# A feed-forward up-projection on TensorE: seven half-size block products in place of eight for 19 of 22 feature tiles

## The chip, the cores and the metric

The kernel runs on one core of one Trainium2 chip. The metric is the device time of one execution in microseconds (us), the median over runs. TensorE (PE in the profile) multiplies, VectorE (DVE), ScalarE (ACT) and GpSimd (POOL) do elementwise work, and SyncE (SP) issues the DMAs.

## The reference, cut to what matters

Two layers, each a token mixer and then a gated feed-forward network (FFN), over 1024 tokens of 1024 features. Only the FFN changes, and in it the first matrix product:

```
def conv_ffn(x, w_in, b_in, conv_w, conv_b, w_out, b_out):
    h = x @ w_in + b_in                      # 1024 x 1024 by 1024 x 5632
    hp = jnp.pad(h, ((0, 0), (1, 1), (0, 0)))
    h = hp[:, :-2] * conv_w[0] + hp[:, 1:-1] * conv_w[1] + hp[:, 2:] * conv_w[2] + conv_b
    u, g = jnp.split(h, 2, axis=-1)          # 2816 features each: 22 tiles of 128
    return (u * jax.nn.gelu(g, approximate=False)) @ w_out + b_out
```

Everything is float32. The residual is added and the sum is layer-normalised.

## The kernel before

`build` runs five kinds of stage one after the other, with a barrier of all engines between them: attention, output projection (`output_stage`), FFN (`ffn_stage`, L968), neighbourhood attention, and again output projection and FFN. The FFN stage is run twice, once for each layer, from about 797 us to 1545 us and from about 2200 us to the end.

Precision: each float32 operand is split into a high part rounded to the fp32r type and a low part, the rest. A product is three matmuls: high by high, high by low, low by high. So one output bank of 128x512 takes 3 matmuls for each 128 of the inner dimension.

In `ffn_stage` the input X is held transposed as XTh and XTl: feature blocks k = 0 to 7 on partitions, 1024 tokens along the free dimension. The hidden features come in FT = 22 tiles f of 128, each in two parities: the value u (parity 0) and the gate g (parity 1). The pieces of work are:

* **Up tile** (`up_tile`, L1121, matmul L1131): for one f and one parity, 2 token halves x 8 k x 3 = 48 matmuls of 128x128 by 128x512 into PSUM `ph[parity]`.
* **Split** (`split`, L1064 to L1072, GpSimd): a 512 KB weight tile that a DMA has put into `wraw` is rounded to `wh` (L1069) and subtracted into `wl` (L1071). `hold` makes it keep order.
* **Take** (`take`, ScalarE): L1229 copies `ph` with bias into H, L1233 makes the centre tap of the convolution in C.
* **Conv** (VectorE): L1289 (left tap) and L1294 (right tap) add into C. Then `gate` (ScalarE, L1239, Gelu), product (VectorE, L1307), `high` (ScalarE, L1243) and `low` (VectorE, L1311) make the two parts Ah and Al of the activation.
* **Down** (`down`, L1134, matmul L1145): for two tiles f at once, 16 output banks r of 6 matmuls each, into four PSUM banks `po` in turn. VectorE adds each bank to X (L1282). TensorE waits before bank r until bank r - 4 has been added.

The order is written out by hand for each engine; the engines meet only at semaphores and each takes its own list in order. On TensorE: tiles of f = 0 and 1, then nine rounds of (both tiles of f = 2i+2, down(i), both tiles of f = 2i+3), then f = 20 and 21, then `down_four` (L1155), which does the last four f at once. Ahead of the rounds ScalarE rescales X (8 instructions, L1221) and GpSimd adds a bias to X (8 instructions, L1079), put between the splits. All VectorE instructions named conv, product, low read two operands from SBUF; the adds of L1282 read one from PSUM and one from SBUF.

Of the kernel before, what the change touches and what calls it, by code (L numbers as in the profile page):

```python
# [9 lines left out]

# [20 lines left out]
class Mem:  # L31
# [11 lines left out]
    def sb(self, name, shape, dt=F32):  # L43
        return self.ctx.enter_context(self.nc.sbuf_tensor(f"{self.prefix}_{name}", shape, dt))

# [649 lines left out]
class Norm:  # L695
# [9 lines left out]
    def __init__(self, nc, m, X, g, b, XTh, XTl, ident, turned_psum, finished):  # L705
# [3 lines left out]
        self.gb = m.sb("gb", [P, 2, self.D])  # L709
# [258 lines left out]
def ffn_stage(nc, name, w_in_d, b_in, conv_w, conv_b, w_out, b_out, g, b, x_out, X, XTh, XTl, ident, alpha, last_layer,  # L968
              wraw, WH, WL, next_tiles):
# [8 lines left out]
    KT, TT, FT = D // P, X.shape[1], FF // P  # L978
    S = TT * P
    G = FT // 2  # L980
    NT = 2 * FT
    with ExitStack() as ctx:  # L982
        m = Mem(nc, ctx, name)
        CUT = 2
        wh, wl = WH[:, 0:4], WL[:, 0:4]
        Ah, Al = WH[:, 4:8], WL[:, 4:8]
        prefetch = None if last_layer else Prefetch(m, wraw, next_tiles)
        H = m.sb("H", [P, 2, S + 2])
        C = m.sb("C", [P, 2, S])
        prow = m.sb("prow", [NT, 5, P])  # L990
        par = m.sb("par", [P, 5, NT])
        centre = m.sb("centre", [P, 2, NT])
        bias = m.sb("bias", [P, D])
        ph = [m.ps(f"ph{i}", [P, KT, P]) for i in range(2)]
        po = [m.ps(f"po{i}", [P, BANK]) for i in range(4)]
        FINISHED = (TT - 1,)
        norm = Norm(nc, m, X, g, b, XTh, XTl, ident, ph, FINISHED)
        wt_in = [m.sem(f"wt_in{i}") for i in range(2)]
        w_high, w_low = m.sem("w_high"), m.sem("w_low")
        par_in, par_turned, par_set, pads_set, bias_in = (m.sem(s) for s in ("par_in", "par_turned", "par_set", "pads_set", "bias_in"))  # L1000
        up_done, up_out, conv_link, conv_done, gated, prod_ready, a_high, a_low = (
            m.sem(s) for s in ("up_done", "up_out", "conv_link", "conv_done", "gated", "prod_ready", "a_high", "a_low"))
        down_done, added, pool_passed = m.sem("down_done"), m.sem("added"), m.sem("pool_passed")
        centre_step = m.sem("centre_step")
        rescaled, biased = m.sem("rescaled"), m.sem("biased")
        y_stored = [m.sem(f"y_stored{i}") for i in range(2)]
        block = ctx.enter_context(nc.Block())
        LAST_SLOTS = (1, 2, 0, 1, 2, 0, 3, 1)
        OUTS = TT * (D // BANK)
        EARLY = 8  # L1010

        def last_bank(r):

            return po[r % 4] if r < 4 or r >= EARLY else ph[(r - 4) // 2][:].rearrange("p k n -> p (k n)")[:, (r % 2) * BANK:(r % 2 + 1) * BANK]

        @block.sync
        def _(sp):
            sp.dma_start(prow[:, 0], b_in.rearrange("(t p) -> t p", p=P)).then_inc(par_in, 16)
            sp.dma_start(prow[:, 1:4], conv_w.rearrange("c (t p) -> t c p", p=P)).then_inc(par_in, 16)
            sp.dma_start(prow[:, 4], conv_b.rearrange("(t p) -> t p", p=P)).then_inc(par_in, 16)  # L1020

            def up(w, slot, f, gate, first=False):
                if not first:
                    sp.wait_ge(w_low, w - 1 - CUT)
                sp.dma_start(wraw[:, slot].rearrange("p (k n) -> p k n", k=KT),
                             column_tile(w_in_d, f * P + gate * FF)).then_inc(wt_in[slot], 16)

            def down(w, slot, f):
                sp.wait_ge(w_low, w - 1 - CUT)
                sp.dma_start(wraw[:, slot], w_out[bass.ds(f * P, P), :]).then_inc(wt_in[slot], 16)  # L1030

            for j in range(CUT, 4):
                up(j, j % 2, j // 2, j % 2, True)
            sp.dma_start(bias[:], b_out.rearrange("(o d) -> o d", o=1).to_broadcast([P, D])).then_inc(bias_in, 16)
            norm.load(sp)
            with sp.Fori(0, G - 2) as i:
                w = 6 * i + 4
                up(w, 0, 2 * i + 2, 0)
                up(w + 1, 1, 2 * i + 2, 1)
                down(w + 2, 0, 2 * i)  # L1040
                down(w + 3, 1, 2 * i + 1)
                up(w + 4, 0, 2 * i + 3, 0)
                up(w + 5, 1, 2 * i + 3, 1)
            w = 6 * G - 8
            for j in range(4):
                up(w + j, j % 2, FT - 2 + j // 2, j % 2)
            for j in range(4):
                down(w + 4 + j, j % 2, FT - 4 + j)
            if prefetch:
                sp.wait_ge(w_low, 6 * G - CUT)  # L1050
                prefetch.start(sp)
                prefetch.wait(sp)
            for t in range(TT):
                norm.wait_y(sp, t)
                sp.dma_start(x_out[t * P:(t + 1) * P, :], X[:, t]).then_inc(y_stored[t % 2], 16)
            for i in range(2):
                sp.wait_ge(y_stored[i], 16 * (TT // 2))

        @block.gpsimd
        def _(pool):  # L1060
# [3 lines left out]
            def split(w, uses, raw_slot, slot):  # L1064

                pool.wait_ge(wt_in[raw_slot], 16 * (uses - 1))
                if not (isinstance(w, int) and w == CUT):
                    hold(pool, w_low, w - CUT, pool_passed)
                nc.gpsimd.tensor_scalar(wh[:, slot], wraw[:, raw_slot], 1.0, 1.0, ALU.mult, ALU.mult).then_inc(w_high, 1)  # L1069
                pool.wait_ge(w_high, w + 1 - CUT)  # L1070
                nc.gpsimd.tensor_tensor(out=wl[:, slot], in0=wraw[:, raw_slot], in1=wh[:, slot].bitcast(F32),  # L1071
                                        op=ALU.subtract).then_inc(w_low, 1)  # L1072

            def add_bias(t):
# [4 lines left out]
                nc.gpsimd.tensor_tensor(out=X[:, t], in0=X[:, t], in1=bias[:], op=ALU.add).then_inc(biased, 1)  # L1079

            for w in range(CUT, 4):
                if w == 3:
                    pool.wait_ge(up_done, 1)
                split(w, w // 2 + 1, w % 2, w % 3)

            def round_(i, first):
                w = 6 * i + 4

                for j in range(6):
                    if first and j < 4:  # L1090
                        add_bias(2 * j)
                        add_bias(2 * j + 1)
                    if j == 0:
                        pool.wait_ge(up_done, 4 * i + 2)
                        if not first:
                            pool.wait_ge(down_done, OUTS * i)
                    elif j < 5:
                        pool.wait_ge(up_done, 4 * i + 2 + j)
                    else:
                        pool.wait_ge(down_done, OUTS * i + OUTS)  # L1100
                    split(w + j, 3 * i + 3 + j // 2, j % 2, (1 + j) % 3)

            round_(0, True)
            with pool.Fori(1, G - 2) as i:
                round_(i, False)
            w = 6 * G - 8
            pool.wait_ge(down_done, OUTS * (G - 2))
            for j, slot in enumerate(LAST_SLOTS):
                if j != 6:
                    pool.wait_ge(up_done, 4 * G - 6 + j if j < 6 else 4 * G)  # L1110
                split(w + j, (w + j) // 2 + 1, j % 2, slot)
# [8 lines left out]
        def _(pe):  # L1120
            def up_tile(a, parity, w, slot, first=False):  # L1121
                if not (isinstance(w, int) and w < CUT):
                    pe.wait_ge(w_low, w + 1 - CUT)
                if not first:
                    pe.wait_ge(up_out, a - 1)
                out = ph[parity][:].rearrange("p k n -> p (k n)")
                for half in range(S // BANK):
                    at = slice(half * BANK, (half + 1) * BANK)
                    for k in range(KT):
                        for n, (wt, x) in enumerate(((wh, XTh), (wh, XTl), (wl, XTh))):  # L1130
                            last = nc.tensor.matmul(out[:, at], wt[:, slot, k * P:(k + 1) * P], x[:, k, at],  # L1131
# [3 lines left out]
            def down(i, w, slots, first):  # L1135

                pe.wait_ge(w_low, w + 2 - CUT)
                pe.wait_ge(a_low, 2 * i + 2)
                for r in range(OUTS):
                    t, half = r // 2, r % 2  # L1140
                    if not first or r >= 4:
                        pe.wait_ge(added, OUTS * i + r - 3)
                    for f in range(2):
                        for n, (a, wt) in enumerate(((Ah, wh), (Ah, wl), (Al, wh))):
                            last = nc.tensor.matmul(po[r % 4][:], a[:, f, t * P:(t + 1) * P],  # L1145
                                                    wt[:, slots[f], half * BANK:(half + 1) * BANK],
                                                    start=(f == 0 and n == 0), stop=(f == 1 and n == 2))
                    last.then_inc(down_done, 1)

            def four_products(r, f0, n):  # L1150

                t, half = r // 2, r % 2
                for f in range(f0, f0 + n):
                    for j, (a, wt) in enumerate(((Ah, wh), (Ah, wl), (Al, wh))):
                        last = nc.tensor.matmul(last_bank(r)[:], a[:, f, t * P:(t + 1) * P],  # L1155
# [781 lines left out]
```

## Time and profile before

| what | value |
|---|---|
| median of 3 runs | 2939.55 us (2937.84 to 2942.13) |
| the profiled execution, its own time | 2941.45 us |
| its span from first to last instruction | 2939.6 us |
| mean granted TensorE clock | 0.975 |
| PE busy | 2761.2 us (94%) |
| DVE busy | 1646.7 us (56%) |
| POOL busy | 1244.3 us (42%) |
| ACT busy | 993.7 us (34%) |

The busy share of PE counts each matmul from its start to its modelled end, and these overlap, so the share says that PE is rarely without work and not how fast it goes. The pace is read from the chain of waits instead: a stretch of matmuls with its count and its length.

### The profile page before, as it was taken

How to read it: one execution, taken by the hardware profiler on the slowest of the kernel's cores; microseconds unless marked ns; L12 is line 12 of the kernel's file. 1: busy time of each engine (PE TensorE's matmuls, PEld its weight loads, DVE VectorE, ACT ScalarE, POOL GpSimd, SP SyncE). 2: the span in 40 equal slices, each digit the busy share in tenths (PEclk: the TensorE clock that was granted, in tenths of full speed). 3: DMA queues.
4: the chain of work that ended last, by engine and by line, in shares of the span. 5: the costliest groups of instructions: out<-in, count | busy, mean ns of one | idle time of the engine just before them, and what ended most of it. 6: DMA issues, size and time to landing. Idle time of an engine off the chain costs nothing. (4 is left out here: it accounts for less than half of the span.)

```text
span 2939.6 us, 36441 instructions
## 1 busy us (share of the span) xinstructions
PE 2761.2 (94%) x13387; PEld 2300.0 (78%) x13387; DVE 1646.7 (56%) x2106; ACT 993.7 (34%) x1402; POOL 1244.3 (42%) x890
## 2 busy tenths in 40 slices
PE   7999999967899999999988999998789999999998
PEld 6788888856788888888877888887668888888886
DVE  3666666663564444444473777777475444444447
ACT  3544555442231122222233555555323111222222
POOL 2444444333563333333354566555357233333335
PEclk9999999988999999999999999999899999999999
DMA  3000001225111111111121221211602111111111
GB/s 117 26 27 24 29 29 35 56 67 190 41 47 43 51 54 46 50 48 45 50 79 42 64 51 44 48 44 22 213 13 75 43 43 52 55 43 50 50 43 72
DMA packets 212649, 163.16 MB, mean 56 GB/s; under 512 B 34939, under 2 KB 194251, under 8 KB 212555
## 3 DMA queue, kind: packets, MB, share of 16 engines
q1 hardware_dynamic: 212411, 161.38, 18.6%
q8 instruction: 59, 0.97, 0.1%
q10 hardware_dynamic: 144, 0.52, 0.1%
q14 instruction: 35, 0.29, 0.0%
HBM read 137.24 MB, written 24.64 MB: 55 GB/s over the span
## 5 line engine op out<-in xcount | busy, mean ns | idle before, releaser
L1131 PE MATMUL ff_ph<-XTh,WH 128*128 128x512 f32 x1408 | 549.7, 390 | 6.9 <-PEq L41 6.9
L1131 PE MATMUL ff_ph<-XTl,WH 128*128 128x512 f32 x1408 | 548.9, 390 | 0.0
L1131 PE MATMUL ff_ph<-XTh,WL 128*128 128x512 f32 x1408 | 548.7, 390 | 0.0
L1289 DVE SCALAR_TENSOR_TENSOR ff_C<-ff_H,ff_par,ff_C 128x1024 f32<-128x1024 f32 x88 | 206.5, 2346 | 548.1 <-ACT ff_C L1233 548.1
L1069 POOL TENSOR_SCALAR WH<-raw_weights 128x1024 fp32r<-128x1024 f32 x128 | 142.3, 1111 | 845.6 <-PE ff_ph L1131 488.9
L1071 POOL TENSOR_TENSOR WL<-raw_weights,WH 128x1024 fp32r<-128x1024 f32 x128 | 328.9, 2570 | 10.7
L1131 PEld LDWEIGHTS ff_ph<-XTh,WH 128*128 128x128 f32 x1408 | 265.0, 188 | 62.7 <-issue 7.6
L1131 PEld LDWEIGHTS ff_ph<-XTh,WL 128*128 128x128 f32 x1408 | 265.0, 188 | 55.5
L1131 PEld LDWEIGHTS ff_ph<-XTl,WH 128*128 128x128 f32 x1408 | 265.1, 188 | 54.9
L1229 ACT ACTIVATE ff_H<-ff_ph,ff_par 128x1024 f32<-128x1024 f32 x88 | 98.4, 1118 | 553.6 <-PE ff_ph L1131 553.6
L1282 DVE TENSOR_TENSOR X<-ff_po,X 128x512 f32<-128x512 f32 x288 | 191.6, 684 | 102.5 <-PE ff_po L1145 102.5
L1145 PE MATMUL ff_po<-WH 128*128 128x512 f32 x576 | 228.3, 396 | 4.7 <-DVE X L1282 0.2
L1145 PE MATMUL ff_po<-WH,WL 128*128 128x512 f32 x576 | 224.4, 390 | 0.0
L1145 PE MATMUL ff_po<-WL,WH 128*128 128x512 f32 x576 | 224.4, 390 | 0.0
L547 ACT ACTIVATE da_E<-da_S,da_mn 128x1024 f32<-128x1024 f32 x128 | 142.9, 1117 | 226.4 <-DVE da_mn L660 223.7
L1526 POOL TENSOR_SCALAR na_E<-na_E,na_rden 128x512 f32<-128x512 f32 x128 | 103.8, 811 | 204.8 <-DVE na_rden L1868 204.7
L1612 PE MATMUL na_pa<-XTh,na_wh 128*128 128x512 f32 x360 | 146.1, 406 | 18.8 <-ACT na_raw L1731 11.8
L278 POOL TENSOR_SCALAR da_E<-da_E,da_rden,da_neglam 128x1024 f32<-128x1024 f32 x64 | 76.6, 1197 | 199.6 <-DVE da_rden L674 199.6
L347 PE MATMUL da_pa<-XTh,da_wh 128*128 128x512 f32 x360 | 151.7, 421 | 10.0 <-POOL da_wl L272 3.8
L660 DVE CUSTOM_DVE_ANT_0 da_S<-da_S,da_strip 128x1024 f32<-128x1024 f32 x128 | 153.8, 1241 | 9.2 <-PE da_S L361 8.2
L1243 ACT ACTIVATE WH<-ff_C 128x1024 fp32r<-128x1024 f32 x44 | 46.8, 1063 | 306.5 <-PE ff_po L1145 268.9
L1612 PE MATMUL na_pa<-XTl,na_wh 128*128 128x512 f32 x360 | 143.9, 400 | 0.0
(224 smaller groups left out, 5990.7 us busy)
## 6 DMA issues: line engine op xcount, KB each, us to landing
raw_weights<-in_ffn_w_in SPq DMA_DIRECT2D x88, 512.0 KB, 3.8
raw_weights<-in_ffn_w_out SPq DMA_DIRECT2D x44, 512.0 KB, 3.5
raw_weights<-in_attn_w_qkv SPq DMA_DIRECT2D x24, 512.0 KB
raw_weights<-in_na_w_qkv SPq DMA_DIRECT2D x24, 512.0 KB, 4.2
wo_oraw<-heads_t SPq DMA_DIRECT2D x16, 512.0 KB, 4.6
rpb_rows<-da_rows SPq DMA_DIRECT2D x2, 3840.0 KB, 26.4
na_B<-rpb_rows SPq DMA_DIRECT2D x32, 224.0 KB, 4.2
da_E<-in_x SPq DMA_DIRECT2D x8, 512.0 KB, 6.5
```

The source lines that it names most:

```text
L347: last = nc.tensor.matmul(out[:], w[:, j // 2, k], x[:, k, t0:t0 + BANK], start=(i == 0), stop=(i == 3 * KT - 1))
L547: nc.scalar.activation(E[:, t % 2, c], Sc[c][:], ACT.Exp, scale=-1.0, bias=mn[:, t % 2, c:c + 1], accum_out=den[:, t % 2, c:c + 1]).then_i ...
L660: nc.vector.tensor_tensor_reduce(out=Sc[c][:], in0=Sc[c][:], in1=strip[:, (QT - 1 - t) * P:(QT - 1 - t) * P + S], scale=1.0, scalar=3.0e38 ...
L1069: nc.gpsimd.tensor_scalar(wh[:, slot], wraw[:, raw_slot], 1.0, 1.0, ALU.mult, ALU.mult).then_inc(w_high, 1)
L1071: nc.gpsimd.tensor_tensor(out=wl[:, slot], in0=wraw[:, raw_slot], in1=wh[:, slot].bitcast(F32), op=ALU.subtract).then_inc(w_low, 1)
L1131: last = nc.tensor.matmul(out[:, at], wt[:, slot, k * P:(k + 1) * P], x[:, k, at], start=(k == 0 and n == 0), stop=(k == KT - 1 and n == 2))
L1145: last = nc.tensor.matmul(po[r % 4][:], a[:, f, t * P:(t + 1) * P], wt[:, slots[f], half * BANK:(half + 1) * BANK], start=(f == 0 and n == ...
L1229: nc.scalar.activation(H[:, parity, 1:S + 1], ph[parity][:].rearrange("p k n -> p (k n)"), ACT.Identity, bias=par[:, 0, bass.ds(idx, 1)])
L1282: nc.vector.tensor_tensor(out=at, in0=po[r % 4][:], in1=at, op=ALU.add).then_inc(added, 1)
L1289: nc.vector.scalar_tensor_tensor(out=c, in0=h[:, 0:S], scalar=tap[1], in1=c, op0=ALU.mult, op1=ALU.add).then_inc(conv_link, 1)
L1526: nc.gpsimd.tensor_scalar(E[:, b], E[:, b], rden[:, b:b + 1], 1.0, ALU.mult, ALU.mult).then_inc(scaled, 1)
L1612: last = nc.tensor.matmul(out[:], w[:, j // 2, k], x[:, k, t0:t0 + BANK], start=(i == 0), stop=(i == 3 * KT - 1))
```

## The change

f = 0, 1, 2 are done as before (`up_plain`). For f = 3 to 21 both parities are computed together by Strassen's scheme. The 2x2 blocks are: parity (value, gate) by token half for the output, inner half k = 1, 2 by token half for X, parity by inner half for the weights. A weight quarter is 128 x 512. Seven products M5, M2, M1, M3, M4, M7, M6 of 4 x 3 = 12 matmuls each replace eight. The sums of X blocks are made once for each layer (B1, B3, B4 and B7 by VectorE, B6 by GpSimd). The sums of weight quarters are made for each f by GpSimd (`quad_add`), rounded by ScalarE (`quad_copy`) and subtracted by GpSimd (`quad_lower`), in four slots of a ring, Rh and Rl; index i of a product uses slot i mod 4. The quarters come by four DMAs of 256 KB (`piece`). VectorE and ScalarE put the products together into H (`sum_u`, `cross_take`, `main_prepare`, `main_take`, `keep`, `centre_tap`). The rounding of a `w_out` tile goes from GpSimd to ScalarE (`down_copy`), its low part stays on GpSimd (`down_lower`). All loops are written out. The order of TensorE is now f = 0, 1, 2, down(0), and then f = 3, 4, down(1), f = 5, 6, down(2) and so on to f = 17, 18, down(8), and f = 19, 20, 21, down_four. The core of the diff:

```
+    PLAIN = 3
+    SLOTS = 4
+    M5, M2, M1, M3, M4, M7, M6 = range(7)
+    SUMS = {M5: 1, M2: 2, M1: 3, M7: 4, M6: 5}
...
+            def piece(f, gate, k):
+                n = f - PLAIN
...
+                    sp.wait_ge(quad_sum, 5 * (n - 1) + (5 if k == 1 else 4))
...
+                sp.dma_start(quad(gate, k).rearrange("p (k n) -> p k n", k=HK), src).then_inc(piece_in[2 * gate + k - 1], 16)
+            def pieces(f):
+                piece(f, 0, 2)
+                piece(f, 1, 2)
+                piece(f, 0, 1)
+                piece(f, 1, 1)
...
+            def quad_add(f, j):
...
+                a, b, op = {M5: ((0, 1), (0, 2), ALU.add), M2: ((1, 1), (1, 2), ALU.add), M1: ((0, 1), (1, 2), ALU.add),
+                            M7: ((0, 2), (1, 2), ALU.subtract), M6: ((1, 1), (0, 1), ALU.subtract)}[j]
...
+                    pool.wait_ge(made, i - SLOTS + 1)
+                nc.gpsimd.tensor_tensor(out=Rf[:, i % SLOTS], in0=quad(*a), in1=quad(*b), op=op).then_inc(quad_sum, 1)
...
+            def next_quads(f):
+                quad_add(f, M5)
+                quad_add(f, M2)
+                quad_lower(f, M5)
+                quad_add(f, M1)
+                quad_lower(f, M2)
+                quad_lower(f, M1)
+                quad_lower(f, M3)
+            for t in range(4):
+                add_bias(t)
+            split(2)
+            split(3)
+            for t in range(4, TT):
+                add_bias(t)
+            for f in range(2):
+                down_lower(f)
+            split(4)
+            split(5)
+            next_quads(PLAIN)
+            pool.wait_ge(up_done, 2 * PLAIN)
...
+            for f in range(PLAIN, FT):
+                quad_lower(f, M4)
+                quad_add(f, M7)
+                if f < FT - 1:
+                    down_lower(f - 1)
+                quad_add(f, M6)
+                quad_lower(f, M7)
+                quad_lower(f, M6)
+                if f + 1 < FT:
+                    next_quads(f + 1)
...
+            def multiply(f, j, out):
+                i = index(f, j)
+                pe.wait_ge(quad_low, i + 1)
...
+            def down(i):
+                pe.wait_ge(down_low, 2 * i + 2)
+                pe.wait_ge(a_low, 2 * i + 2)
...
         @block.scalar
...
+            mix_copy(B1)
+            take(0)
+            mix_copy(B3)
+            take(1)
+            gate(0)
+            high(0)
+            down_copy(0)
+            down_copy(1)
+            take(2)
+            mix_copy(B4)
+            take(3)
...
+            for f in range(PLAIN, FT):
+                behind_down = f % 2 == 1 and f < FT - 1
+                if behind_down:
+                    high(f - 1)
+                keep(f, M5)
+                quad_copy(f, M4)
+                keep(f, M2)
+                quad_copy(f, M7)
+                if f < FT - 1:
+                    down_copy(f - 1)
+                if f == PLAIN:
+                    mix_copy(B7)
+                quad_copy(f, M6)
+                if f + 1 < FT:
+                    quad_copy(f + 1, M5)
+                if not behind_down:
+                    gate(f - 1)
+                if f + 1 < FT:
+                    quad_copy(f + 1, M2)
+                if not behind_down:
+                    high(f - 1)
+                if f + 1 < FT:
+                    quad_copy(f + 1, M1)
+                centre_tap(f, 0)
+                if f + 1 < FT:
+                    quad_copy(f + 1, M3)
+                centre_tap(f, 1)
+                if f % 2 == 0 and f < FT - 2:
+                    gate(f)
...
         @block.vector
...
+            mix_sums(B1)
+            mix_sums(B3)
...
+            mix_lower(B1, 1)
+            left(0, 0), right(0, 0)
+            mix_lower(B3, 2)
+            left(0, 1), right(0, 1)
+            product(0)
+            low(0)
+            dve.wait_ge(up_done, 2)
+            mix_sums(B4)
+            left(1, 0), right(1, 0)
+            mix_lower(B4, 3)
...
+            for f in range(PLAIN, FT):
...
+                if not behind_down:
+                    left(f - 1, 0), right(f - 1, 0)
...
+                if not behind_down:
+                    left(f - 1, 1)
+                sum_u(f)
...
+                if not behind_down:
+                    right(f - 1, 1)
+                cross_take(f, 0)
+                main_prepare(f, 1)
+                if not behind_down:
+                    product(f - 1)
+                cross_take(f, 1)
+                main_prepare(f, 0)
+                if not behind_down:
+                    low(f - 1)
+                main_take(f, 0)
+                main_take(f, 1)
+                if f % 2 == 0 and f < FT - 2:
+                    done = OUTS * (f // 2 - 1)
+                    left(f, 0), add(done), add(done + 1)
+                    right(f, 0), add(done + 2), add(done + 3)
+                    left(f, 1), add(done + 4), add(done + 5)
+                    right(f, 1)
...
```

The first part of the diff is SyncE's, from `quad_add` on it is GpSimd's, from `multiply` on TensorE's. Behind GpSimd's wait for `2 * PLAIN` stand three adds and one subtraction of 128x2048 for B6, with a ScalarE copy ahead of the last. `mix_copy(B1)` stands behind the rescaling of X; `mix_sums` is three 128x2048 adds or subtractions, `mix_lower` one. `quad_lower` waits for `quad_copy` of the same index; `quad_copy` of a sum waits for its `quad_add`. `sum_u`, `cross_take`, `main_prepare` and `main_take` read one operand from PSUM and one from SBUF, 512 elements each.

## Rows read from the trace of the kernel before

**Rows 1.** The page: busy time of the engines, and the granted clock by slice.
```profile
PE 2761.2 (94%) x13387; PEld 2300.0 (78%) x13387; DVE 1646.7 (56%) x2106; ACT 993.7 (34%) x1402; POOL 1244.3 (42%) x890
PEclk9999999988999999999999999999899999999999
```

**Rows 2.** Chain of waits, second FFN: start us, length us, what.
```profile
2199.60 12.62 PE ff_ph L1131 x48
2212.66 54.64 PE ff_ph L1131 x240
...
2289.84 43.53 PE ff_ph L1131 x192
...
2340.72 15.27 PE ff_po L1145 x66
2355.99 43.53 PE ff_ph L1131 x192
...
2818.97 65.28 PE ff_ph L1131 x288
2884.25 5.44 PE ff_po L1155 x24
```

**Rows 3.** Timeline, 2399 to 2405 us: start, length, engine, line, operation.
```profile
2399.34 0.39 PE L1145 MATMUL ff_po<-WH 128*128 128x512 f32 x1
2399.65 1.12 ACT L1229 ACTIVATE ff_H<-ff_ph,ff_par 128x1024 f32<-128x1024 f32 x1 [8.60 <-PE ff_ph L1131]
2400.95 2.39 POOL L1071 TENSOR_TENSOR WL<-raw_weights,WH 128x1024 fp32r<-128x1024 f32 x1
2402.00 2.42 DVE L1289 SCALAR_TENSOR_TENSOR ff_C<-ff_H,ff_par,ff_C 128x1024 f32<-128x1024 f32 x1 [7.10 <-ACT ff_C L1233]
2404.95 1.27 DVE L1294 SCALAR_TENSOR_TENSOR ff_C<-ff_H,ff_par,ff_C 128x1024 f32<-128x1024 f32 x1
```

**Rows 4.** Timeline, start of the second FFN, DVE and then POOL.
```profile
2226.10 3.41 DVE L1289 SCALAR_TENSOR_TENSOR ff_C<-ff_H,ff_par,ff_C 128x1024 f32<-128x1024 f32 x1
2229.55 3.30 DVE L1294 SCALAR_TENSOR_TENSOR ff_C<-ff_H,ff_par,ff_C 128x1024 f32<-128x1024 f32 x1
...
2225.19 3.24 POOL L1071 TENSOR_TENSOR WL<-raw_weights,WH 128x1024 fp32r<-128x1024 f32 x1
2228.39 6.71 POOL L1079 TENSOR_TENSOR X<-X,ff_bias 128x1024 f32<-128x1024 f32 x2
```

**Rows 5.** One line each: durations in ns, least/median/most.
```profile
L1071 POOL TENSOR_TENSOR WL<-raw_weights,WH x128: 2388/2400/3337, 803.1 to 2885.6; 128x1024 fp32r<-128x1024 f32 x128
L1510 POOL TENSOR_TENSOR na_B<-na_colmask,na_B x16: 2114/2420/3091, 1556.8 to 2047.6; 128x896 f32<-128x896 f32 x16
L1282 DVE TENSOR_TENSOR X<-ff_po,X x288: 671/691/692, 869.1 to 2819.0; 128x512 f32<-128x512 f32 x144
L1307 DVE TENSOR_TENSOR ff_C<-ff_C x44: 1205/1224/2216, 831.0 to 2891.5; 128x1024 f32<-128x1024 f32 x44
L1069 POOL TENSOR_SCALAR WH<-raw_weights x128: 1047/1052/2037, 802.0 to 2884.5; 128x1024 fp32r<-128x1024 f32 x128
```

**Rows 6.** Groups of instructions: busy us, mean ns of one, idle before.
```profile
L490 ACT ACTIVATE da_raw<-da_pa 128x512 f32<-128x512 f32 x45 | 26.8, 596 | 36.8 <-PE da_pa L347 36.8
L1239 ACT ACTIVATE ff_C<-ff_C 128x1024 f32<-128x1024 f32 x44 | 46.7, 1060 | 190.4 <-DVE ff_C L1294 190.4
```

**Rows 7.** DMA issues: KB each, median us from issue to landing.
```profile
raw_weights<-in_ffn_w_in SPq DMA_DIRECT2D x88, 512.0 KB, 3.8
heads_t<-da_ostage SPq DMA_DIRECT2D x32, 128.0 KB, 1.8
```

**Rows 8.** Timeline, start of the second FFN, ScalarE and then GpSimd.
```profile
2213.08 7.70 ACT L1221 ACTIVATE X<-X 128x1024 f32<-128x1024 f32 x8
2220.68 1.10 ACT L1229 ACTIVATE ff_H<-ff_ph,ff_par 128x1024 f32<-128x1024 f32 x1
...
2216.00 4.78 POOL L1079 TENSOR_TENSOR X<-X,ff_bias 128x1024 f32<-128x1024 f32 x2
```

More of the change, by code:

```diff
@@ L1103, in _ @@
[L1103 to L1111, printed above, removed]
+                nc.gpsimd.tensor_tensor(out=X[:, t], in0=X[:, t], in1=bias, op=ALU.add).then_inc(biased, 1)
@@ L1120, in _, with up_plain @@
         def _(pe):
[L1121 to L1124, printed above, removed]
+            def up_plain(a):
+                if a >= 2:
+                    pe.wait_ge(w_low, a - 1)
                     pe.wait_ge(up_out, a - 1)
-                out = ph[parity][:].rearrange("p k n -> p (k n)")
+                high, low = (WH[:, a], WL[:, a]) if a < 2 else (tile_slot(0, a), tile_slot(1, a))
                 for half in range(S // BANK):
@@ L1133, in up_tile @@
                 last.then_inc(up_done, 1)
-            def down(i, w, slots, first):
-                pe.wait_ge(w_low, w + 2 - CUT)
+            def multiply(f, j, out):
+                i = index(f, j)
+                pe.wait_ge(quad_low, i + 1)
+                xh, xl = moving[j]
+                for k in range(HK):
+                    wh, wl = (part[:, i % SLOTS, k * P:(k + 1) * P] for part in (Rh, Rl))
+                    for n, (w, x) in enumerate(((wh, xh), (wh, xl), (wl, xh))):
+                        last = nc.tensor.matmul(out, w, x[:, k], start=(k == 0 and n == 0),
+                                                stop=(k == HK - 1 and n == 2))
+                last.then_inc(made, 1)
@@ new lines, in products @@
+            def products(out, r, f0, n, first, last_f):
+                t, half = r // 2, r % 2
+                for f in range(f0, f0 + n):
+                    (ah, al), (wh, wl, _) = a_slot(f), d_slot(f)
+                    for j, (a, w) in enumerate(((ah, wh), (ah, wl), (al, wh))):
+                        last = nc.tensor.matmul(out, a[:, t * P:(t + 1) * P], w[:, half * BANK:(half + 1) * BANK],
+                                                start=(f == first and j == 0), stop=(f == last_f and j == 2))
+                return last
@@ L1138, in down @@
+            def down(i):
+                pe.wait_ge(down_low, 2 * i + 2)
                 pe.wait_ge(a_low, 2 * i + 2)
                 for r in range(OUTS):
-                    t, half = r // 2, r % 2
-                    if not first or r >= 4:
+                    if i or r >= 4:
                         pe.wait_ge(added, OUTS * i + r - 3)
[L1143 to L1155, printed above, removed]
-                                                wt[:, LAST_SLOTS[4 + f], half * BANK:(half + 1) * BANK],
-                                                start=(f == 0 and j == 0), stop=(f == 3 and j == 2))
-                return last
@@ L1262, in _ @@
+            down_copy(FT - 2)
+            down_copy(FT - 1)
+            gate(FT - 1)
+            high(FT - 1)
             for t in range(TT):
@@ new lines, in _ @@
+            mix_lower(B1, 1)
[8 more added lines that the diff above has]
+            mix_lower(B4, 3)
+            left(1, 1), right(1, 1)
+            dve.wait_ge(biased, TT)
+            product(1)
+            low(1)
+            left(2, 0), right(2, 0)
+            left(2, 1), add(0), add(1), right(2, 1)
@@ L1331, in add_last @@
+            f = FT - 1
+            left(f, 0), right(f, 0), left(f, 1), right(f, 1)
+            product(f)
+            low(f)
             def add_last(r):
```

565 lines of the change are left out of this document (381 added, 184 removed).

## The prediction

> **What bounds the kernel now.** I read the page first [rows 1]: PE is busy 94% of the span at nearly the full granted clock, no other engine over 56%. Busy time of PE overlaps, so the pace comes from the chain of waits [rows 2]: 192 matmuls in 43.53 us, 0.2267 us each, and both FFN stages run at that pace almost without a break. The same chain gives the round: up tiles start at 2289.84 and at 2355.99, 66.15 us apart. Of that 43.53 us are two f of 96 matmuls, 21.76 us (96 x 0.2267) is the down product, and 0.85 us is lost at its fifth and sixth bank, where the add comes late. So TensorE sets the time, and what the change takes from it is worth its full price unless another list falls behind.
>
> **What the change takes from TensorE.** 84 matmuls stand in place of 96: 12 x 0.2267 = 2.72 us for each f, 51.7 us for 19 f, 103.4 us for two layers. One f costs PE 19.05 us, a product of 12 matmuls 2.72 us.
>
> **What it adds elsewhere.** GpSimd does for each f five sums and seven low parts of 128x512 and one low part of 128x1024. A GpSimd TENSOR_TENSOR of 1024 takes 2.39 us and one of 896 takes 2.11 [rows 5]; the line through both gives 1.29 us at 512, half of the longer gives 1.20, and I take 1.29 (bounds 1.15 and 1.40). That is 12 x 1.29 + 2.4 = 17.9 us in 19.05, without a wait. It can't be spread: a slot of the ring is free only when the product four places back is done.
>
> **The port.** GpSimd and VectorE hold each other up. VectorE's left tap starts at 2402.00 and ends at 2404.42, 1.08 us after GpSimd's subtraction has ended at 2403.34; the right tap by itself takes 1.27 [rows 3]. At the start of the stage, with both queues full, the two alternate: each VectorE tap takes 3.3 us and each GpSimd add 3.36 instead of 2.4 [rows 4]. So a VectorE instruction with two SBUF operands puts 0.95 us (3.36 - 2.4) into GpSimd's list, and the whole GpSimd instruction into its own. Adds from PSUM show no such stretch: 671 to 692 ns over 288 [rows 5]. Of the new VectorE work only taps, product, low and the X-block sums pay this toll; `sum_u` and the takes read PSUM.
>
> **A pair of f, step by step.** Zero is where TensorE starts M5 of odd f = o; e = o+1; four products stand ready. TensorE alone would end e at 38.1. ScalarE copies: 512 elements 0.60, 1024 elements 1.06 [rows 6]; each hop between engines 0.1; from TensorE 0.31, as the start of the next matmul at 2399.34 and of ScalarE at 2399.65 show [rows 3].
> * M5 and M2 end, 5.44 + 0.31 = 5.75, which frees the slot of M7. GpSimd adds M7: 7.04.
> * ScalarE copies it (0.7) and does `down_copy` (1.06): 8.80. `down_lower`, standing next in GpSimd's list, 2.5: 11.30. Sum of M6, 1.29: 12.59.
> * Only that sum frees the quarters (value, 1) and (gate, 1) for their DMAs. 512 KB land in 3.8 us, 128 KB of a store in 1.8 [rows 7]: 2.6 for 256 KB (bounds 1.8 and 3.8), and 0.2 of hops: 15.39.
> * Six GpSimd instructions of `next_quads` for e, 7.74: 23.13.
> * VectorE's taps of o are due now (M1's copy is done at 21.2, `centre_tap` at 22.3). The low parts of M3 and M4 and the sum of M7 each let one tap pass: 3 x (0.95 + 1.29) = 6.72: 29.85.
> * Copy of M7, `down_copy`, `down_lower`, sum of M6: 0.7 + 1.06 + 2.5 + 1.29 = 5.55: 35.40. The low part of M7 ends at 36.7, where TensorE has been waiting since about 33. M7 and M6 end at 42.2.
> * DMA again, 2.8: 38.20. Sum of the next M5, 39.49. ScalarE copies it, 40.19, and only then reaches the Gelu of o, which stands behind it: 41.25.
> * Product of o: asks at 41.35, gets the port at 42.07, done 43.1. `high` 44.3. `low` gets the port behind two GpSimd instructions at 45.63, done 46.65. The down product needs it: TensorE starts at 46.75, not at 38.1.
> * Down 21.76. The adds keep up: left tap of e done at 49.9, first two adds by 51.1, and bank 4 is due at 52.1.
>
> The pair takes 68.5 us where the round took 66.15: 8.7 us of waits eat the 5.44 us saved and the 0.85. From the end of down(0) to `down_four` the kernel before needs 21.8 + 8 x 66.15 + 43.5 = 594.5 us (its last 288 matmuls are the 65.28 us of [rows 2]). After: 8 x 68.5 = 548, and f = 19, 20, 21 in a row. These three are 57.2 us of TensorE; f = 20 waits 3.7 us as above, f = 21 has no `down_lower` ahead and waits some 3: 64. Sum 612, that is +17.5 us a layer.
>
> **The start of the stage.** The list of GpSimd now has four bias adds ahead of the second pair of splits. The first rescaled tile is there 14.5 us into the stage [rows 8], four adds make it 24.1, the low part of B1 (128x2048 on VectorE, about 2.0 of port by twice the row of 1224 ns in [rows 5]) 26.1, split(2) with one tap between (1.05 + 0.95 + 2.4) 30.5. TensorE wants it at 24.0 (2212.66 + 10.9 [rows 2]). From there both lists are full: GpSimd's up to split(4) is one split, four bias adds, two `down_lower`, one split, 3.45 + 9.6 + 4.8 + 3.45 = 21.3; VectorE's in the same stretch six instructions of 1024 (5.7) and four of 2048 (8.0). The sum is 65.5, where TensorE starts tile 4 that it would start at 45.6. With two tiles (21.8) the down product starts at 87.3, before at 67.7 (2212.66 + 54.64): +19.6, less 0.85 for the adds. Then B6, four GpSimd instructions of 2048 at 4.8 and a copy, ends about 6 us into the next pair; low(2) and three B7 sums on VectorE pass between. The sum of M6 of f = 3 stands at 19 us of the pair instead of 12.6: +6.4. Together +25 us a layer.
>
> **Sum.** 17.5 + 25 + about 1 at the end (the last f has taps, Gelu, product, high and low in 10.9 us of TensorE's work) = 43.5 a layer, 87 for two. The profiled execution's own time is 2941.45 us, 1.9 above the median: 2939.55 + 87 gives 3027. Nothing outside the FFN changes. Writing out the loops I cost at nothing: the 192 matmuls in 43.53 us [rows 2] span a loop's end, at the pace of the stretches within a loop's body. If fetching the longer code costs, it is not in this sum; no row bounds it.
>
> Only a page has another price for the GpSimd subtraction: by the Trainium skill (GPSIMD Engine Reference, "Elementwise — side-by-side cycle accounting"), 2.6 cycles an element, 512 elements are an estimated 1.11 us. With it the pair would be about 66.2 us, the same as the round before; the line through the two rows says 1.29 and stands above that.
>
> **The rivals.**
> * *Everything is hidden.* The lists keep up and only TensorE's 103 us count: 2836 us. For it: average loads (GpSimd 17.9 of 19.05, in a pair even 36 of 60). Against it: the low part of o hangs on a DMA, a sum, two copies and a Gelu in line, and the chain would have to be 8.6 us shorter. Chance 0.10.
> * *The port costs little or the small instructions are short.* With no wait for the port the three insertions (2.85) and the waits of product and low (1.8) go: 63.9 a pair, -2.3 x 8; -1.3 for the last three; the start loses 4 (the bias adds alone) and 3 (B6): -12.6 a layer, 2914 us. For it: VectorE's rows alone don't tell how short GpSimd instructions of 512 share. Against: rows 4 show alternation. Chance 0.17, and it reaches up to no change (0.04 of it).
> * *TensorE's gaps cost clock too.* Where PE now waits, in the attention stages, slices show 0.8 to 0.9 granted [rows 1]. At 0.94 in both FFN stages, 6% of some 1200 us of matmuls: 3100 us. Against: waits of 4 us between stretches of 20 to 30. Chance 0.08.
> * The forecast itself, GpSimd's chain and the port set the pair: slower. Chance 0.65, with 2975 to 3080 as its range: DMA landing 0.8 less or 1.2 more twice a pair, GpSimd 0.1 less or more in a dozen instructions.
>
> No change is within 0.2%, about 6 us. Faster: 0.10 + 0.13 and a little of the forecast's lower end, 0.25. Same 0.05. Slower 0.70. The range is 2900 to 3085.
>
> **What would show it.** In the profile after: TensorE waits before M7 of even f for GpSimd's `quad_lower`, and before each down product from down(1) on for VectorE's `low`, 4 to 5 us each; down(0) starts 87 us into the stage; GpSimd's 512 instructions 1.29 us alone and 2.2 against a tap; the pair 68.5. The prediction is wrong if the pair is under 66 us, or if tile 4 starts before 55 us, or if the low of odd f ends before TensorE's M6.

## The result and the profile after

| | before | after | forecast |
|---|---|---|---|
| median of 4 runs, us | 2940.84 (2937.84 to 2944.07) | 3071.08 (3065.67 to 3076.27) | 3027 |
| after / before | | 1.044 (95% interval 1.0425 to 1.0452) | 1.030 |
| profiled span, us | 2939.6 | 3063.9 | |
| mean granted TensorE clock | 0.975 | 0.946 | |

The page after, answering to [rows 1]: busy time by engine, and the granted TensorE clock by slice. PE's instructions fall by 456 (19 x 12 x 2), GpSimd's busy time grows by 423 us and VectorE's by 322.

```profile
PE 2731.1 (89%) x12931; PEld 2258.3 (74%) x12931; DVE 1968.3 (64%) x2446; ACT 1171.2 (38%) x1722; POOL 1667.3 (54%) x1158
PEclk9999999979898999999999999998989899999999
```

The chain of waits after (start us, length us, what), one pair of f (an odd f, the even f behind it and a down product) in the second FFN and the start of the next one. It answers to the three-line round of [rows 2], which held only PE:

```profile
2453.14 5.45 PE ff_ph L1280 x24
2458.75 1.29 POOL ff_Rlf L1191
2460.04 1.66 issue
2461.74 2.39 POOL ff_WDl L1205
...
2473.51 6.98 POOL ff_Rl L1198 x4
2480.49 2.23 POOL ff_Rlf L1191
2482.73 1.66 issue
2484.43 2.38 POOL ff_WDl L1205
...
2489.40 8.57 PE ff_ph L1280 x24
2497.97 1.50 issue
2499.47 22.01 PE ff_po L1324 x96
2521.48 5.45 PE ff_ph L1280 x24
```

Between two products of TensorE (M5 and M2 of the odd f, and M7 and M6 of the even f) the chain runs through GpSimd alone: L1191 is a sum, L1198 a low part, L1205 the low part of a w_out tile, and each 1.66 "issue" is GpSimd waiting for ScalarE's copy ahead of L1205. The pair takes 68.34 us (2521.48 - 2453.14), the next one 68.43. Of the last seven pairs of this stage five take 68.3 to 68.7 us, and two take 71.0 and 71.2.

GpSimd's sums, durations in ns, least/median/most, as in [rows 5]:

```profile
L1191 POOL TENSOR_TENSOR ff_Rlf<-raw_weights x190: 1257/1292/3338, 875.4 to 2993.3; 128x512 f32<-128x512 f32 x190
```

The timeline of the even f, ScalarE and then VectorE. The Gelu (L1403) comes right behind a copy (L1436) that had waited 3.65 us for a sum; VectorE has nothing to do for 8.39 us:

```profile
2492.34 0.63 ACT L1436 ACTIVATE ff_Rh<-ff_Rlf 128x512 fp32r<-128x512 f32 x1 [3.65 <-POOL ff_Rlf L1191]
2492.88 1.04 ACT L1403 ACTIVATE ff_C<-ff_C 128x1024 f32<-128x1024 f32 x1
...
2493.95 1.92 DVE L1573 TENSOR_TENSOR ff_C<-ff_C 128x1024 f32<-128x1024 f32 x1 [8.39 <-ACT ff_C L1403]
```

Where the second FFN's 62 us come from. The stage is 740.0 us before (2199.6 to 2939.6) and 802.0 after (2261.9 to 3063.9). Each stretch runs from TensorE's first matmul of one part to its first of the next; the last three f are 19 to 21, and the rest begins with `down_four`:

| stretch | before | after | more | forecast |
|---|---|---|---|---|
| stage start to down(0) | 67.5 | 89.7 | +22.2 | +19.6 |
| down(0) | 22.6 | 21.8 | -0.7 | -0.85 |
| first pair | 66.1 | 79.5 | +13.4 | +8.8 |
| seven pairs | 463.0 | 484.7 | +21.7 | +16.5 |
| last three f | 65.3 | 64.8 | -0.5 | -1.3 |
| the rest | 55.5 | 61.4 | +5.9 | +1 |

The first FFN stage after repeats it: 90.2, 21.8, 81.0, 484.8 and 64.7 us down to `down_four`.

### The profile page after: what moved, and what is told of

Its sections match the earlier page's. It is cut to its first block and busy times, and to the rows that moved or that the text cites. A ratio compares the mean times of both kernels' runs of the same rounds, so it can differ in the third digit from the quotient of the medians.

```text
span 3063.9 us, 35380 instructions
## 1 busy us (share of the span) xinstructions
PE 2731.1 (89%) x12931; PEld 2258.3 (74%) x12931; DVE 1968.3 (64%) x2446; ACT 1171.2 (38%) x1722; POOL 1667.3 (54%) x1158
## 5 line engine op out<-in xcount | busy, mean ns | idle before, releaser
L1198 POOL TENSOR_TENSOR ff_Rl<-raw_weights,ff_Rh 128x512 fp32r<-128x512 f32 x76 | 145.6, 1924 | 388.0 <-ACT ff_Rh L1436 388.0
L1280 PE MATMUL ff_ph<-XTh,ff_Rh 128*128 128x512 f32 x608 | 258.6, 425 | 74.1 <-POOL ff_Rl L1198 55.0
L1191 POOL TENSOR_TENSOR ff_Rlf<-raw_weights 128x512 f32<-128x512 f32 x190 | 288.9, 1529 | 57.1 <-PE ff_ph L1268 26.5
L1324 PE MATMUL ff_po<-ff_WDh,WH 128*128 128x512 f32 x624 | 250.9, 402 | 42.1 <-issue 42.1
L1436 ACT ACTIVATE ff_Rh<-ff_Rlf 128x512 fp32r<-128x512 f32 x190 | 119.7, 630 | 415.6 <-POOL ff_Rlf L1191 413.9
L1198 POOL TENSOR_TENSOR ff_Rl<-ff_Rlf,ff_Rh 128x512 fp32r<-128x512 f32 x190 | 268.3, 1429 | 0.8 <-ACT ff_Rh L1436 0.4
L1554 DVE TENSOR_TENSOR X<-ff_po,X 128x512 f32<-128x512 f32 x288 | 194.1, 686 | 91.3 <-PE ff_po L1324 91.3
L1280 PE MATMUL ff_ph<-XTl,ff_Rh 128*128 128x512 f32 x608 | 251.9, 414 | 0.0
L1280 PE MATMUL ff_ph<-XTh,ff_Rl 128*128 128x512 f32 x608 | 250.7, 412 | 0.0
L1324 PE MATMUL ff_po<-ff_WDh,WL 128*128 128x512 f32 x624 | 248.4, 398 | 0.0
L1324 PE MATMUL ff_po<-ff_WDl,WH 128*128 128x512 f32 x624 | 248.3, 398 | 0.0
L1562 DVE SCALAR_TENSOR_TENSOR ff_C<-ff_H,ff_par,ff_C 128x1024 f32<-128x1024 f32 x88 | 158.6, 1802 | 66.2 <-ACT ff_C L1453 47.8
L1280 PE MATMUL ff_ph<-WH,ff_Rh 128*128 128x512 f32 x456 | 177.4, 389 | 0.0
L1280 PE MATMUL ff_ph<-WL,ff_Rh 128*128 128x512 f32 x456 | 177.4, 389 | 0.0
```

What stands on the lines that cost most here:

```text
L1191: nc.gpsimd.tensor_tensor(out=Rf[:, i % SLOTS], in0=quad(*a), in1=quad(*b), op=op).then_inc(quad_sum, 1)
L1198: nc.gpsimd.tensor_tensor(out=Rl[:, i % SLOTS], in0=src, in1=Rh[:, i % SLOTS].bitcast(F32), op=ALU.subtract).then_inc(quad_low, 1)
L1280: last = nc.tensor.matmul(out, w, x[:, k], start=(k == 0 and n == 0), stop=(k == HK - 1 and n == 2))
L1324: last = nc.tensor.matmul(out, a[:, t * P:(t + 1) * P], w[:, half * BANK:(half + 1) * BANK], start=(f == first and j == 0), stop=(f == las ...
L1436: nc.scalar.activation(Rh[:, i % SLOTS], src, ACT.Copy).then_inc(quad_high, 1)
L1554: nc.vector.tensor_tensor(out=at, in0=po[r % 4][:], in1=at, op=ALU.add).then_inc(added, 1)
```

## The experiments

All keep 84 matmuls for each f from 3 on. Ratios are to the kernel before, run on the same chip in the same series.

**Gelu and rounding earlier (e_gate).** ScalarE only:

```
                 if f == PLAIN:
                     mix_copy(B7)
+                if not behind_down:
+                    gate(f - 1)
                 quad_copy(f, M6)
+                if not behind_down:
+                    high(f - 1)
                 if f + 1 < FT:
                     quad_copy(f + 1, M5)
-                if not behind_down:
-                    gate(f - 1)
...
-                if not behind_down:
-                    high(f - 1)
```

> ScalarE alone is reordered: the Gelu of the tile before stands ahead of the copy of M6, and its rounding (high) ahead of the copy of the next M5. Theory (lists in order, GpSimd and the port): the low part of the odd tile is then early, TensorE's wait before the down product goes, and the down product starts where M6 ends. M7 still starts 36.3 us into the pair, so the pair is 36.3 + 8.5 (M7 and M6 at the lowered clock) + 22.0 = 66.8 us instead of 68.4; if the lowered clock is not owed to the wait before M7, 63.8. Time about 3045 us. Rival (TensorE is slow for another reason: clock or code fetch): no change, 3071.

Measured 3023.57 us, ratio 1.028 (1.0261 to 1.0295). The chain of this kernel, one pair and the start of the one after the next:

```profile
2433.36 5.45 PE ff_ph L1280 x24
2470.75 7.13 PE ff_ph L1280 x24
2477.88 21.76 PE ff_po L1324 x96
2499.64 5.46 PE ff_ph L1280 x24
...
2566.82 5.45 PE ff_ph L1280 x24
```

The wait ahead of the down product is gone, and its 96 matmuls go at full pace. Pairs of 66.28 and 67.18 us stand where 66.8 was expected; M7 starts at 37.4 us of the pair, 1.1 later. The total is 21 us less than expected. The trace of the second FFN shows where: the seven pairs take 467.4 us instead of 484.7, 17.2 less where 11 were expected; the first pair takes 74.9 instead of 79.5, and the last three f 63.6 instead of 64.8.

**Low part of w_out later (e_dlow).** GpSimd only:

```
                 quad_add(f, M7)
-                if f < FT - 1:
-                    down_lower(f - 1)
                 quad_add(f, M6)
                 quad_lower(f, M7)
                 quad_lower(f, M6)
+                if f < FT - 1:
+                    down_lower(f - 1)
```

> GpSimd alone is reordered: down_lower stands behind the low part of M6, no longer ahead of the sum of M6. Theory: the sum of M6 and the quarters' DMAs come 4.1 us earlier (2.4 of the subtraction and 1.7 of waiting for its ScalarE copy), M7 of the even tile is ready when TensorE comes (33 us), and the low part of the odd tile, still behind the DMA, a sum and the Gelu, lets the down product start at 43.5 instead of 46.3: pair 65.3 us, or up to 68 if the now longer wait in one piece lowers the clock in the down product. Time 3020 to 3065 us. Rival (the DMA of the quarters is the limit): the wait before M7 stays.

Measured 3045.11 us, ratio 1.035 (1.0333 to 1.0368). The chain:

```profile
2416.85 24.93 PE ff_po L1324 x96
2441.77 38.11 PE ff_ph L1280 x168
2479.88 6.05 issue
```

All 14 products run in 38.11 us, and the next down product starts at 2485.93, so the wait before M7 is gone; what was a wait in two pieces is one of 6 us ahead of the down product, and that takes 24.93 us in the line shown and 24.0 to 24.4 in the later pairs. The pair is 69.1 here and 68.3 to 68.7 later, a little over the upper end of what was expected for it; the total lies inside its range. Either reordering alone is worth little of the 8 us of waits.

**Both (e_both).** The two edits together.

> Both reorderings. Theory: no list is later than TensorE any more; the pair is 19.05 x 2 + 22 = 60.1 to 61 us, against 66.15 of the round before and 68.4 of the change. 16 pairs at 7.5 less and a few us from the last three tiles: 2940 to 2955 us, what is left above the 2838 us of a hidden change is the start of the stage (about 35 us a layer) and its end (6). Rival (GpSimd and the port lack throughput, whatever the order): a pair of 65 or more.

Measured 3006.20 us, ratio 1.022 (1.0203 to 1.0237): over the expected range by 51 us, and in the rival's favour by its number. The chain of one pair says why:

```profile
2466.82 1.26 POOL ff_Rlf L1191
...
2468.64 1.24 ACT ff_C L1453
...
2469.90 1.72 DVE ff_C L1562
2471.61 0.61 DVE X L1554
...
2472.27 19.51 PE ff_po L1324 x72
2491.78 32.66 PE ff_ph L1280 x144
...
2557.24 32.66 PE ff_ph L1280 x144
```

The pair is 65.46 us. The products go unhindered (32.66 us for 144 matmuls), but now TensorE waits up to 3.3 us in each down product: bank 4 of the down product waits for VectorE's first add (L1554), that for the left tap (L1562), that for ScalarE's centre tap (L1453), and that, in ScalarE's list, for the copy of the next M1 behind GpSimd. In the change this wait doesn't show: there the down product itself starts late.

**Start of GpSimd's list as well (e_all).** e_both, and at the start of the stage GpSimd does split(2) and split(3) first, six bias adds, split(4), two bias adds, split(5), then the low parts.

> Both reorderings and GpSimd's list at the start: split(2) and split(3) ahead of the bias adds, split(4) ahead of the last two, split(5) next, down_lower(0) and (1) behind them. Theory: tile 2 starts at 25 to 27 us of the stage instead of 38, tile 4 at about 48 to 55 instead of 66; the down product of tiles 0 and 1 is then bound by VectorE's list (X-block sums against the port) and starts at 75 to 82 instead of 90. So 8 to 15 us a layer less than with both reorderings alone: 2910 to 2935 us, below the kernel before.

Measured 2998.26 us, ratio 1.019 (1.0175 to 1.0209). 8 us for two layers where 16 to 30 were expected: TensorE now waits 20.8 us in five places for ScalarE's take (L1398) ahead of plain up tiles, where the change waited 34.6 us in four places for GpSimd's split (L1170). That the take in its turn waits for VectorE's list, so that the reordering only moved work within a full queue, is the reading; no run here isolates it.

**Centre taps first (e_tap).** e_both, and for even f with a down product behind them:

```
+                early = f % 2 == 0 and f < FT - 2
+                if early:
+                    centre_tap(f, 0)
+                    centre_tap(f, 1)
                 if f + 1 < FT:
                     quad_copy(f + 1, M5)
```

> Both reorderings, and for even f that a down product follows, ScalarE does the two centre taps ahead of the four copies for the next f. Theory: what holds the pair of e_both at 65.5 us is bank 4 of the down product, whose add stands behind a tap of VectorE, that behind the centre tap of ScalarE, and that behind the copy of the next M1, which needs GpSimd. With the centre tap first the adds come in time and the pair is 60.1 to 60.5 us. 16 pairs at 5.4 less: about 2920 us, under the kernel before. Rival (GpSimd's load and the port limit the pair at about 65): 3006 us as before.

Measured 2920.80 us, ratio 0.993 (0.9915 to 0.9948), as expected: 0.7% faster than the kernel before.

```profile
2427.40 38.13 PE ff_ph L1280 x168
2465.64 22.12 PE ff_po L1324 x96
2487.77 38.10 PE ff_ph L1280 x168
```

The pair is 60.37 us (2487.77 - 2427.40), and TensorE alone needs 59.84 (e_empty below). Of the 8.5 us of waits in the change's pair 8.0 go by order alone, with every instruction kept: in the pairs GpSimd and the port had the throughput.

**A new start (e_best).** e_tap, and VectorE does scaling and bias in one instruction for each of the eight token blocks, in place of ScalarE's eight and GpSimd's eight; in VectorE's list some neighbours of these instructions change places too. ScalarE's order there is copies of B1 and B3, the two w_out tiles, then the takes.

```
-            for t in range(4):
-                add_bias(t)
             split(2)
             split(3)
-            for t in range(4, TT):
-                add_bias(t)
             for f in range(2):
                 down_lower(f)
...
+                nc.vector.scalar_tensor_tensor(out=X[:, t], in0=X[:, t], scalar=alpha, in1=bias, op0=ALU.mult,
+                                               op1=ALU.add).then_inc(biased, 1)
```

> The kernel of e_tap with a new start: VectorE scales X and adds the bias in one instruction of 1.28 us (8 of them), in place of ScalarE's 8 and GpSimd's 8 of 2.4 us; GpSimd's list is split(2), split(3), down_lower(0) and (1), split(4), split(5); ScalarE copies B1, B3 and the first two w_out tiles while TensorE does tile 0. Theory (the start is a queue at the shared port): 19.2 us of GpSimd go and 7.6 us of port come for them; the down product of tiles 0 and 1 starts at 70 to 78 us of the stage instead of 90, so 12 to 20 us a layer less than e_tap: 2880 to 2900 us. Rival (the start is slow for TensorE's clock): no gain over e_tap.

Measured 2885.74 us, ratio 0.981 (0.9796 to 0.9829), inside its range: 56 us under the kernel before of the same series, the best of all here. Its down(0) starts at 2238.9, 69.9 us into a stage that starts at 2169.0, against 89.7.

**GpSimd's sums and low parts nearly empty (e_empty).** Left out as the expectation says, ScalarE's copies of the sums with them, so this run does not tell GpSimd's time from theirs. The change's own order; two executions.

```
-                nc.gpsimd.tensor_tensor(out=Rf[:, i % SLOTS], in0=quad(*a), in1=quad(*b), op=op).then_inc(quad_sum, 1)
+                nc.gpsimd.tensor_tensor(out=Rf[:, i % SLOTS, 0:8], in0=quad(*a)[:, 0:8], in1=quad(*b)[:, 0:8], op=op).then_inc(quad_sum, 1)
```

> The order of the change is kept. Left out: GpSimd's sums, ScalarE's copies of them and GpSimd's low parts cover 8 columns instead of 512. TensorE, the taps, the X-block sums and the low parts of w_out are whole. Theory (GpSimd's time in the chain): pairs at TensorE's own 60.1 to 61 us, the start still some 20 us late a layer: 2915 to 2940 us. Rival (TensorE loses to its clock, to code fetch or to the new access patterns of its operands): pairs at 66 or more.

Measured 2887.36 us, ratio 0.981 (0.9794 to 0.9833), 28 us under the expected range. The chain is PE alone, 38.08 + 21.76 = 59.84 us a pair, and the last three f take 57.13. The first pair gains most beyond what was expected: it takes 60.6 us where the change takes 79.5.

```profile
2407.34 38.08 PE ff_ph L1280 x168
2445.42 21.76 PE ff_po L1324 x96
...
2766.38 57.13 PE ff_ph L1280 x252
```

**Taps nearly empty (e_taps).** The left tap, and the right one in the same way; two executions:

```
+                w = S if f < PLAIN else 8
-                nc.vector.scalar_tensor_tensor(out=C[:, parity], in0=H[:, parity, 0:S], scalar=par[:, 1, idx:idx + 1],
-                                               in1=C[:, parity], op0=ALU.mult, op1=ALU.add).then_inc(conv_link, 1)
+                nc.vector.scalar_tensor_tensor(out=C[:, parity, 0:w], in0=H[:, parity, 0:w], scalar=par[:, 1, idx:idx + 1],
+                                               in1=C[:, parity, 0:w], op0=ALU.mult, op1=ALU.add).then_inc(conv_link, 1)
```

> The order of the change is kept. Left out: the left and right taps of VectorE cover 8 columns instead of 1024 for f from 3 on. Theory: the three tap instructions that get the port between GpSimd's put 2.85 us into the chain of a pair; without them the pair is 65.3 us, about 3015 us in all. Rival (the port costs nothing, GpSimd's own work is all): 68.4 and 3065.

Measured 3027.70 us, ratio 1.029 (1.0270 to 1.0311). One pair:

```profile
2437.64 5.45 PE ff_ph L1280 x24
2471.86 5.70 PE ff_ph L1280 x24
2482.02 23.62 PE ff_po L1324 x96
2505.65 5.45 PE ff_ph L1280 x24
```

M7 starts at 34.2 us instead of 36.3. GpSimd's list of the two kernels, after and then e_taps, shows the price of the port and what stands behind it:

```profile
2475.99 4.51 POOL L1198 TENSOR_TENSOR ff_Rl<-raw_weights,ff_Rh 128x512 fp32r<-128x512 f32 x2
2480.46 2.27 POOL L1191 TENSOR_TENSOR ff_Rlf<-raw_weights 128x512 f32<-128x512 f32 x1
```

```profile
2460.55 1.31 POOL L1198 TENSOR_TENSOR ff_Rl<-raw_weights,ff_Rh 128x512 fp32r<-128x512 f32 x1
2462.62 1.29 POOL L1198 TENSOR_TENSOR ff_Rl<-raw_weights,ff_Rh 128x512 fp32r<-128x512 f32 x1 [0.76 <-ACT ff_Rh L1436]
2463.87 1.28 POOL L1191 TENSOR_TENSOR ff_Rlf<-raw_weights 128x512 f32<-128x512 f32 x1
```

Three instructions take 6.78 us with the taps and 3.88 without, 2.9 us for three insertions; 0.76 of it comes back as a wait for ScalarE's copy, which leaves the 2.1 us of M7. The pair is 68.0 all the same, by its number the rival's: the down product takes 23.6 us instead of 22.0. So the two lists show the price of the port, and the pair's length does not. Of the 43 us gained in all the seven pairs of a stage give 7.5 (477.2 us instead of 484.7), the first pair 2.1, the last three f 5.0 and the end 6.1, that is 20.7 a stage: the forecast of 3015 was near for reasons that it did not have.

**The new start with the change's order (e_start2).** The edit of e_best alone, without those of e_gate, e_dlow and e_tap.

> Only the start of e_best (scaling and bias on VectorE, GpSimd's list without the bias adds), with the order of the change in every later f. Theory (start and pairs are two separate queues whose prices add): the 35 us by which e_best is under e_tap come here too, 3071 - 35 = 3036 us (3026 to 3046); the pairs stay at 68.4. Rival (the first pair takes back what the start gives, as it waits for B6 and B7): 3060 or more.

Measured 3039.78 us, ratio 1.033 (1.0315 to 1.0350): 31 us less than the change, where 35 were expected; down(0) starts 69.9 us into the stage, as in e_best. Start and pairs add.

**The quarters loaded once (e_dma).**

```
             def pieces(f):
+                if f > PLAIN:
+                    return
...
-                    pool.wait_ge(piece_in[2 * gate + k - 1], 16 * (n + 1))
+                    pool.wait_ge(piece_in[2 * gate + k - 1], 16)
```

> The order of the change. Left out: the DMAs of the weight quarters for f from 4 on; the sums are made of the quarters of f = 3. Theory: the DMA stands in the chain twice a pair, but two low parts of GpSimd (2.58 us) lie beside it, so only the 0.55 us in which GpSimd waits for the landing goes, 1.1 us a pair: 67.3 us, 3050 us in all. Rival (the DMA's 2.8 us counts in full): 62.8 a pair, 2980 us.

Measured 3053.72 us, ratio 1.038 (1.0364 to 1.0401), 17 us less, where 21 were expected. The chain, one pair:

```profile
2443.88 5.45 PE ff_ph L1282 x24
...
2488.99 23.46 PE ff_po L1326 x96
2512.45 5.45 PE ff_ph L1282 x24
```

The down product starts at 45.1 us of the pair, 1.2 earlier, as expected: the DMAs of the quarters lie beside GpSimd's low parts. This pair is 68.6 us none the less, as the slow stretch lies in the down product (23.46 us); so the total agrees and the 67.3 us of a pair do not. The rival's 62.8 us a pair is far off.

## Why the prediction was right, and where it was short

The direction, the place and the mechanism came out: GpSimd's list, the port and a Gelu that stands behind a late sum make the pair longer. The size was short by 44 of 130 us. Some 5 of the 44 are not in the traces (the profiled execution after took 3065.67 us, the median is 3071.08); 18 are in the second FFN and much the same in the first. None of the three signs of a wrong prediction showed: the pair is not under 66 us, tile 4 starts at 66.1 us of the stage (forecast 65.5), and the low part of the odd f ends behind TensorE's M6.

* **TensorE's saving** (103.4 us): right. e_empty runs 84 matmuls in 19.04 us and its pairs at full pace.
* **The pair**: forecast 68.5, measured 68.34 in the pair shown, and 69.2 in the mean of seven. Step by step, M7 at 36.8 (measured 36.26), the down product at 46.75 (46.33). The GpSimd instruction of 512 was put at 1.29 by a line through two rows and is 1.292 by the median of 190; the lower price of 1.11 that the prediction sets beside it is not what the trace shows. The first sum behind the DMA was put at 15.39 and is at 15.33, in part by luck: the sum ahead of it was 0.3 us earlier than forecast and the DMA with its hops took 3.1 us, not 2.8. Three insertions at the port were put at 2.85 and are 2.9 in the two lists above.
* **ScalarE's Gelu behind a copy behind a sum**: right, and e_gate takes exactly that wait away.
* **The clock is the term that failed.** It was a rival at 0.08 and stands in the sum at nothing, yet the windows view shows 0.95 granted in each of the seven pairs. In the pair shown, after 3.10 us without work, PE runs M7 and the first two matmuls of M6 at the lower level of 1.2 GHz; 24 matmuls take 8.57 us instead of 5.44. The forecast has these 24 end at 42.2 us and a wait of 4.5 behind them; in fact the clock eats 3.1 us of that wait, so in five of the seven pairs it costs nothing. That the pair came out at 68.3 in spite of it is luck in this respect. In the two others the same wait of 3.10 us ahead of M7 is followed by 24 matmuls at full pace (5.69 us), the wait ahead of the down product is then 4.3 and 4.6 us, and the down product behind it is the slow one: 24.67 and 24.65 us instead of 22.01. Nothing hides that, and so seven pairs took 5 us more than forecast. The rival's sum of 3100 us charges the clock in full, which is too much where a wait stands behind the slow stretch.
* **The start**: +22.2 against +19.6, right in kind. Of the 2.6 us missed 1.8 are the clock again: behind a wait of 11 us the two tiles ahead of down(0) take 23.6 us, not 21.8, at a granted clock of 0.92. Down(0) loses its old wait, as forecast: its 96 matmuls run without a break, in 21.8 us.
* **The first pair**: 79.5, forecast 74.9. B6 was right: it ends 6.1 us into the pair (forecast 6), and the sum of M6 of f = 3 stands at 19.3 us (19). B7 had no wait of its own in the forecast. VectorE's product, low and three B7 sums alternate with GpSimd at the port, and TensorE waits for the low part that follows them. The product, and TensorE's first matmul of M7 of f = 3:

```profile
2368.85 5.18 DVE L1573 TENSOR_TENSOR ff_C<-ff_C 128x1024 f32<-128x1024 f32 x1
2396.23 0.76 PE L1280 MATMUL ff_ph<-XTh,ff_Rh 128*128 128x512 f32 x1 [8.99 <-DVE XTl L1536]
```

  GpSimd's low part for the same product ends at 2393.98, so some 2.2 us of this wait are B7's and the rest is the late list of GpSimd, as forecast. In e_empty these sums take 2.29 us each and the wait is 0.46. Behind the wait the clock costs again: 36 matmuls take 10.20 us instead of 8.16, and the down product 23.5 instead of 22.0.
* **The end**, the largest miss in proportion: 5.9 instead of 1. The taps of f = 21 met the two last `down_lower` at the port and took 3.35 and 3.31 us, so TensorE waited 4.30 us, and the 24 matmuls behind that wait took 7.1 us instead of 5.5:

```profile
3006.33 3.35 DVE ff_C L1562
3009.70 3.31 DVE ff_C L1568
...
3017.84 4.54 PE ff_po L1324 x12
```

  I had laid these instructions against 10.9 us of TensorE's work at 1.27 each. That is the alternation of [rows 4], which I had used everywhere but here. In e_taps, without the taps, the wait is gone.
* The miss of 18 us in the second FFN is thus 2.6 (start) + 0.1 (down(0)) + 4.6 (first pair) + 5.2 (pairs) + 0.8 (last three f) + 4.9 (end), all in the same direction. By cause, an estimate from the stretches above: some 12 us are matmuls at the lowered clock with nothing behind them to hide it (1.8 + 3.5 + 5.2 + 1.6), some 6 are the port where the forecast had left it out (B7 2.2, the end 3.3) and tile 4 (0.6).
* **The rival "everything is hidden"** is not what this order of the lists gives, but another order hides nearly all that the pairs cost: e_tap has pairs of 60.4 us. What keeps it from the 2836 us of that rival is, in each stage, some 23 us more at the start, 10 in the first pair, and 12 in the last three f and the end.
* **Code fetch**, left out of the sum: e_empty runs the unrolled code at the full pace of 0.2267 us a matmul, so it costs nothing that shows.

Open: the same wait of 3.10 us is followed by a lowered clock in most pairs and not in all, and no run here shows what decides.

## What to carry to other kernels

Average loads of 17.9 us in 19.05 say neither that work is hidden nor that it isn't: walk the lists in order, because a cheap instruction (a Gelu of 1 us) that stands behind another engine's late one carries the delay to the engine that bounds. Here the same instructions in another order turned 4.4% slower into 0.7% faster, and a new start, with scaling and bias in one instruction of VectorE, gave 1.2% more. When one wait is removed look for the one that it hid: two reorderings gave 65 us together, and with a third it was 150.

## What the runs showed that I had not expected

* A wait of 3.10 us between dense matmuls is followed by 6.6 us at a granted clock of 0.54 in the pair shown. Of the last seven pairs of each FFN stage ten go this way; in the other four the same wait is followed by M7 and M6 at a clock of 1.00, and the slow stretch comes behind the next wait. Rows of the windows view for one pair of each kind, and the down product behind the second (start and end, then for each engine busy us and count, granted clock, DMA share, GB/s):

```profile
2489.40:2496.00 6.60, 6.60 (x17) 5.16 (x18) 2.04 (x2) 2.19 (x4) 5.81 (x5) 0.54 0.26 77
2694.94:2700.63 5.69, 5.69 (x24) 4.40 (x24) 1.20 (x1) 2.10 (x3) 5.24 (x5) 1.00 0.29 85
2704.90:2711.50 6.60, 6.59 (x17) 5.20 (x18) 4.21 (x6) 2.89 (x3) 2.91 (x2) 0.57 0.01 2
```

* In e_taps the waits before M7 were 1.0 us, M7 and M6 took 5.70 us, near full pace, and the slow stretch came behind the wait of 4.4 us instead. In these traces a lowered clock is cheapest where the work behind the wait is itself followed by a wait.
